# RWKV passes in another order, and norm rates kept per token on 128x8

## The reference

```python
    kk = heads(k * k_k)
    kk = kk * lax.rsqrt(jnp.sum(kk * kk, axis=-1, keepdims=True) + 1e-12)
    k = k * (1 + (a - 1) * k_a)
    rh, kh, vh, ah = heads(r), heads(k), heads(v), heads(a)
    decay = jnp.exp(-jnp.exp(heads(w_raw)))

    y = _rwkv7_scan(rh, decay, kh, vh, -kk, kk * ah)
    y = _layer_norm(y, gn_g, gn_b, GN_EPS)
    bonus = jnp.sum(rh * kh * r_k.astype(jnp.float32), axis=-1, keepdims=True) * vh
    y = (y + bonus).reshape(Bsz, T, D_B).astype(p_b.dtype)
    return y * jax.nn.silu(gate)
```

## Time and profile before

| what | us |
|---|---|
| median of 3 runs | 2367.26 (2361.62 to 2368.75) |
| the profiled execution, its own time | 2364.19 |
| its span, from first to last instruction | 2362.5 |
| of which passes 0 to 3 of the RWKV branch | 234.2 to 440.8 |
| PE busy | 2154.4 (91%) |
| DVE busy | 1347.4 (57%) |
| ACT busy | 789.4 (33%) |
| POOL busy | 620.1 (26%) |
| mean granted TensorE clock | 0.962 of full speed |

### The profile page before, as it was taken

One profiled execution on the slowest core, in us unless ns is written; L12 is line 12 of the kernel. 1 busy time (PEld: TensorE's weight loads), 2 busy tenths in 40 slices (PEclk: granted clock), 3 DMA queues, 4 the chain that ended last, 5 costly groups with the idle time before them and its releaser, 6 DMA issues.

```text
span 2362.5 us, 39580 instructions
## 1 busy us (share of the span) xinstructions
PE 2154.4 (91%) x15562; PEld 1559.1 (66%) x15562; DVE 1347.4 (57%) x2348; ACT 789.4 (33%) x1433; POOL 620.1 (26%) x1126
## 2 busy tenths in 40 slices
PE   4998787789998999999989968999998999999996
PEld 4876666565564555555555536888786778888875
DVE  2166666347997444444459986888785333333344
ACT  1334433223111344444310036545454432322223
POOL 0453211040102888888701121111111000000001
PEclk7999899899999999999999978999999999999998
DMA  7321323232444111111116433888886323333320
GB/s 292 99 89 63 109 110 144 110 107 79 159 168 144 44 66 56 50 50 61 57 66 239 164 110 118 247 248 237 249 246 210 96 84 98 98 98 98 98 90 36
DMA packets 105000, 294.56 MB, mean 125 GB/s; under 512 B 12400, under 2 KB 49520, under 8 KB 96240
## 3 DMA queue, kind: packets, MB, share of 16 engines
q1 hardware_dynamic: 92464, 227.02, 29.6%
q0 software_dynamic: 12352, 65.02, 7.3%
HBM read 225.01 MB, written 66.98 MB: 124 GB/s over the span
## 4 chain that ended last, share of the span: by engine, by line
PE 80%; DVE 6%; DMA 6%; ACT 3%; issue 3%; SPq 1%; POOL 0%; ACTq 0%; DVEq 0%; POOLq 0%
PE psum L449 29%; PE psum L1706 7%; PE psum L2358 7%; PE psum L2140 4%; PE psum L2105 4%; PE psum L2522 4%; DMA lags<-const 3%; PE psum L2116 2%; PE psum L1006 2%; PE psum L2183 2%; PE psum L2176 2%; PE psum L2129 2%; PE psum L2716 2%; PE psum L2662 1%; PE psum L283 1%
## 5 line engine op out<-in xcount | busy, mean ns | idle before, releaser
L449 PE MATMUL psum<-split,w_split 128*128 128x512 f32 x1632 | 373.2, 390 | 3.7 <-DVE w_split L431 3.7
L449 PEld LDWEIGHTS psum<-split,w_split 128*128 128x128 f32 x1632 | 307.5, 189 | 68.1 <-DVE w_split L431 4.1
L431 DVE TENSOR_TENSOR w_split<-ring,w_split 128x512 fp32r<-128x512 f32 x188 | 133.1, 708 | 318.5 <-ACT w_split L426 318.2
L1925 POOL TENSOR_TENSOR early<-early 128x8 f32<-128x8 f32 (+6 forms) x672 | 277.1, 412 | 52.8
L426 ACT ACTIVATE w_split<-ring 128x512 fp32r<-128x512 f32 x188 | 118.8, 632 | 349.0 <-PE psum L449 345.7
L1706 PE MATMUL psum<-early,ring 128*128 128x512 f32 (+1 forms) x544 | 176.6, 486 | 0.0
L2358 PE MATMUL psum<-gate,ring 128*128 128x512 f32 (+1 forms) x512 | 165.4, 486 | 1.2 <-issue 1.2
L2522 PE MATMUL psum<-h,u_w 128*128 128x256 f32 (+1 forms) x768 | 149.9, 349 | 14.4 <-ACT u_t L2444 13.7
L449 PE MATMUL psum<-h,w_split 128*128 128x512 f32 x624 | 147.9, 398 | 8.5 <-DVE w_split L431 8.5
L1706 PEld LDWEIGHTS psum<-early,ring 128*128 128x128 f32 x544 | 103.7, 191 | 71.8 <-issue 64.6
L2358 PEld LDWEIGHTS psum<-gate,ring 128*128 128x128 f32 x512 | 97.2, 190 | 69.3 <-issue 62.7
(11 more groups left out here) (413 smaller groups left out, 3709.5 us busy)
## 6 DMA issues: line engine op xcount, KB each, us to landing
ring<-in_s_glu SPq DMA_DIRECT2D x64, 512.0 KB, 3.5
ring<-in_w_mod SPq DMA_DIRECT2D x48, 512.0 KB, 5.2
made_c_pow<-area POOLq DMA_DIRECT2D x16, 1152.0 KB, 5.0
c_pow<-made_c_pow SPq DMA_DIRECT2D x16, 1152.0 KB, 6.6
made_b_pow<-area POOLq DMA_DIRECT2D x16, 1024.0 KB, 4.6
b_pow<-made_b_pow SPq DMA_DIRECT2D x16, 1024.0 KB, 10.2
ring<-in_s_in SPq DMA_DIRECT2D x32, 512.0 KB, 6.6
ring<-in_w_in SPq DMA_DIRECT2D x29, 512.0 KB, 3.5
```

The costliest lines, as they stand in the source:

```text
L431: nc.vector.tensor_tensor(rounded(buffer(u, 1)), source(u), buffer(u, 0), ALU.subtract).then_inc(dve_done, 1)
L449: ins = nc.tensor.matmul(out, rounded(buffer(u, w)[:, ks]), values(x, k), start=(first and k == 0 and n == 0), stop=(last and k == UNIT_K ...
L1925: nc.gpsimd.tensor_tensor(o, a, b, op).then_inc(pool_done, 1)
```

## The change

It has two parts. First, both rates are formed per token. `head_sums_pe` takes the squares as the stationary operand, 128 tokens at a time, and two columns of `block_ones` as the moving one, so that the sums lie with tokens on partitions, 128x8 for all tokens and both heads of a pair. Square root and reciprocal work on 128x8 (`key_rate`, `gn_rate`). `spread_pe` brings the rate back to 64 channels of each head by eight products, with the rate's column broadcast as the stationary operand and the identity as the moving one; DVE reads the result from PSUM. This is done once for each of the four pairs and for each of the two norms.

Second, instructions stand elsewhere. On PE the EARLY rows of a pass's first batch come ahead of the AKT product; the keys' sums come after the first level of U, ahead of the first `dz_pe`; state 3 too; the keys' spread stands where the keys' sums stood; the group norm's spread comes after `chunk_maps_pe`, ahead of the third batch. On ACT the keys' square no longer waits for AKT (the sigmoid now writes `be_cm` and leaves `a_cm`), the keys' root comes ahead of the second level's copies, the group norm's square ahead of a copy of `tm`, and the third batch's copy ahead of the gain. On DVE the bonus products (`prep_rk_dve`) come ahead of the keys, the addition of the first batch ahead of the third level's additions to Z, the first half of the operands ahead of the fourth level's, the small reciprocal of the group norm between `r_read` and `carry`, and `gn_out_dve` moves from the end of a pass to the second level of the next, for pair 2 into `rwkv_last_dve`, behind the fourth split of `mixT`.

```diff
@@ project_pe
                 if job == WD_JOB + 3:
                     prep_k_ss_pe(pe, 0)
+                if job == WD_JOB + 4:
+                    prep_k_spread_pe(pe, 0)
@@ project_dve
                 if FIRST_RAW + p == WD_JOB + 2:
-                    prep_recip_dve(dve, 0, 0)
-                    prep_recip_dve(dve, 0, 1)
+                    prep_rk_dve(dve, 0)
+                    prep_recip_dve(dve, 0)
                     prep_keys_dve(dve, 0)
-                    prep_rk_dve(dve, 0)
@@ new helpers
+        def head_sums_pe(out, src):
+            for tt in range(TT):
+                ins = nc.tensor.matmul(out[:, 2 * tt:2 * tt + 2], src[:, tt * P:(tt + 1) * P], mask("block_ones")[:, 0:P:HEAD],
+                                       start=True, stop=True)
+            return ins
+        def spread_pe(out, rate):
+            for tt in range(TT):
+                for e in range(2):
+                    ins = nc.tensor.matmul(out[half(e), tt * P:(tt + 1) * P],
+                                           rate[:, 2 * tt + e:2 * tt + e + 1].broadcast_to([P, HEAD]), mask("ident"),
+                                           start=True, stop=True)
+            return ins
+        def prep_k_spread_pe(pe, q):
+            pe.wait_ge(*at("rw", q, "k_rate"))
+            spread_pe(bank(6), key_rate[:, 1, :]).then_inc(pe_done, 1)
@@ prep_k_sq_act
-            if q > 0:
-                act.wait_ge(*at("rw", q - 1, "AKT"))
@@ prep_norm_act
-            nc.scalar.activation(kk[:, :], bank(6), ACT.Sqrt, bias=eps[:, 3:4]).then_inc(act_done, 1)
+            nc.scalar.activation(key_rate[:, 0, :], bank(6, 0, 2 * TT), ACT.Sqrt, bias=eps[:, 3:4]).then_inc(act_done, 1)
@@ prep_recip_dve
-            nc.vector.reciprocal(tmp[:, hs], kk[:, hs]).then_inc(dve_done, 1)
+            nc.vector.reciprocal(key_rate[:, 1, :], key_rate[:, 0, :]).then_inc(dve_done, 1)
@@ gn_spread_pe (new), gn_rate_dve (new), gn_scale_dve
+            pe.wait_ge(*at("gn", q, "rate"))
+            spread_pe(bank(4), gn_rate[:, 1, :]).then_inc(pe_done, 1)
+            nc.vector.reciprocal(gn_rate[:, 1, :], gn_rate[:, 0, :]).then_inc(dve_done, 1)
-            nc.vector.reciprocal(gn_rcp[:, :], gn_std[:, :]).then_inc(dve_done, 1)
-            nc.vector.tensor_tensor(y, y, gn_rcp[:, :], ALU.mult).then_inc(dve_done, 1)
+            nc.vector.tensor_tensor(y, y, bank(4), ALU.mult).then_inc(dve_done, 1)
@@ rwkv_last_dve
             for k in range(4):
                 split_dve(dve, "mix_split", mix_split, mixT, k)
+            gn_out_dve(dve, q - 1)
```

More of the change, by code:

```diff
@@ L834, in prep_k_ss_pe @@
             pe.wait_ge(*at("rw", q, "decay_sig"))
-            nc.tensor.matmul(bank(6), mask("block_ones"), tmp[:, :], start=True, stop=True).then_inc(pe_done, 1)
+            head_sums_pe(bank(6), tmp).then_inc(pe_done, 1)
             pe_count.up("rw", q, "k_ss")
+        def prep_k_spread_pe(pe, q):
+            pe.wait_ge(*at("rw", q, "k_rate"))
+            spread_pe(bank(6), key_rate[:, 1, :]).then_inc(pe_done, 1)
+            pe_count.up("rw", q, "k_spread")
         def prep_rk_sum_pe(pe, q):
@@ L904, in prep_scan_dve @@
             dve.wait_ge(*at("rw", q, "decay_sig"))
[L905 removed]
+            nc.vector.tensor_tensor_scan(g_cm[:, :], reset, be_cm[:, :], 0.0, ALU.mult, ALU.add).then_inc(dve_done, 1)
             dve.wait_ge(dve_done, dve_count.up("rw", q, "scanned"))
         def prep_decays_dve(dve, q):
[L909 removed]
+            nc.vector.tensor_tensor(a_cm[:, :], g_cm[:, :], be_cm[:, :], ALU.subtract).then_inc(dve_done, 1)
             dve_count.up()
@@ L1231, in gn_ss_pe, with gn_spread_pe @@
             pe.wait_ge(*at("gn", q, "sq"))
-            nc.tensor.matmul(bank(5), mask("block_ones"), gn_sq[:, :], start=True, stop=True).then_inc(pe_done, 1)
+            head_sums_pe(bank(5), gn_sq).then_inc(pe_done, 1)
             pe_count.up("gn", q, "ss")
+        def gn_spread_pe(pe, q):
+            pe.wait_ge(*at("gn", q, "rate"))
+            spread_pe(bank(4), gn_rate[:, 1, :]).then_inc(pe_done, 1)
+            pe_count.up("gn", q, "spread")
         def gn_centre_dve(dve, q):
@@ L1326, in rwkv_pe @@
                 prep_raw_pe(pe, i + 1)
+            vec_rows_pe(pe, n0, EARLY, *([("vec", n0 - 1, "added")] if n0 > FIRST_GATE else []))
             akt_pe(pe, i)
@@ L1330, in rwkv_pe @@
             u_pe(pe, i, 1)
-            vec_rows_pe(pe, n0, EARLY, *([("vec", n0 - 1, "added")] if n0 > FIRST_GATE else []))
-            dz_pe(pe, i, 1)
+            if prep:
+                prep_k_ss_pe(pe, i + 1)
             if scan:
                 state_pe(pe, i - 1, 3)
+            dz_pe(pe, i, 1)
             vec_rows_pe(pe, n0, LATE)
@@ L1383, in rwkv_act @@
             u_act_(act, i, 1)
+            if prep:
+                prep_norm_act(act, i + 1)
             u_act_(act, i, 2)
             vec_copy_act(act, batches[0])
-            if prep:
-                prep_norm_act(act, i + 1)
             u_act_(act, i, 3)
@@ L1400, in rwkv_act @@
             w_act_(act, i)
-            if prep:
-                prep_tm_act(act, i + 1, 1)
             if scan:
@@ L1405, in rwkv_act @@
             if prep:
+                prep_tm_act(act, i + 1, 1)
                 prep_tm_act(act, i + 1, 2)
@@ L1411, in rwkv_act @@
                 prep_tm_act(act, i + 1, 3)
+            if len(batches) == 3:
+                vec_copy_act(act, batches[2])
             if scan:
                 gn_gain_act(act, i - 1)
-            if len(batches) == 3:
-                vec_copy_act(act, batches[2])
             if i == 0:
@@ L1433, in rwkv_dve @@
                 prep_decays_dve(dve, i + 1)
+            if prep:
+                prep_recip_dve(dve, i + 1)
+            if i > 1:
+                gn_out_dve(dve, i - 2)
             dz_dve(dve, i, 2)
@@ L1465, in rwkv_dve @@
                 gn_scale_dve(dve, i - 1)
-                gn_out_dve(dve, i - 1)
             if len(batches) == 3:
```

57 lines of the change are left out of this document (31 added, 26 removed).

## The result

The changed kernel takes 2340.44 us (median of 4 runs, 2338.34 to 2342.94), the kernel before 2365.38 us (4 runs, the three of the table above and one more). The ratio is 0.9893, with a 95% interval of 0.9874 to 0.9911. The forecast was 2342.2. A second set gave 2339.02 against 2363.60, ratio 0.9888 (0.9866 to 0.9911).

The account below looks back on a forecast made before the run. No engine was taken as full: a pass is a chain through all, its lateness showing as PE waits. Terms -1.4 - 3.0 - 12.3 - 3.9 + 1.7 - 1.7 - 1.4 = -22.0 took 2364.2 to 2342.2 us, range 2332 to 2355.

Parts of the forecast that it names:

- Step 1: End of the projections: two bonus products done while the keys wait for their spread, -1.4 us (bounds 0 and -3.4).
- Step 2: Pass start to second level: ACT's square early, EARLY rows moved into mask waits, -4.2; spreads +1.2; together -3.0 us.
- Step 3: Second to fifth level: PE's waits on vector additions, `tmp`, operands and ahead of y end, -12.3 us (bound -8).
- Step 4: Ends of passes 1 and 2: earlier row copy -5.9, earlier square -1.0, two spreads +3.0; together -3.9 us.
- Step 5: End of pass 3 and tail: tail rows start earlier, -1.2; `gn_out_dve` of pair 2 delays states, +1.4; together +1.7 us.
- Step 6: Last group norm, whose end PE waits for: 3.35 us reciprocal goes, 0.17 and a 1.5 spread come; -1.7 us.
- Step 7: TensorE's clock: pass 1 at 0.94 instead of 0.88 would be 2.9 us shorter; half taken, -1.4 us.
- signs of being wrong: Wrong if PE's AKT, weight or `issue` waits grow over 5 us, a spread exceeds 3, projections' DVE end stays 227.8.
- Rival one: Passes: new waits for weights and where rows run into products take back a third, +9 us, 2351; chance 0.18.
- Rival two: Passes: more gain, clock staying up (7 us) and spreads overlapping, -10.5 us, 2332; chance 0.12.
- Rivals three and five: Three: spread far dearer, +38, 2380, chance 0.03; five: weight stream paces passes, only Step 1 and Step 6 left, 2361, 0.04.
- rival four: Spreads: each new change of array mode costs the last product's length, 12 changes, +2.4 us, 2344.6; chance 0.05.

Follow-up runs that it names:

- rates alone: Kernel before with its old instruction order, both rates on 128x8 and spread; 2348.3 us, ratio 0.9904.
- AKT wait back: Changed kernel with one wait put back: ACT's square of the keys waits for AKT as before; 2346.6 us, ratio 0.9927.
- EARLY rows back: Changed kernel with the EARLY rows of a pass's first batch behind the keys' sums, ahead of the first `dz_pe`; 2337.7 us, ratio 0.9875.
- order alone: Kernel before with every engine's instructions in the new order, both rates at full size, no spread; 2338.6 us, ratio 0.9882.
- second profile: Profile of the changed kernel run once more without an edit; median 2339.0 us, ratio 0.9888, profiled execution 2330.8 us.

## Why the prediction was right

The median came within 2 us of the forecast, the profiled execution within 4, and this is partly luck. The change was put at 22.0 us; it is 24.9 by the medians and 25.9 between the two profiles. The terms it had for the waits held, but errors larger than this difference cancelled around them. Gains of some 16 us were missing: 8.6 of clock, 4.7 of waits for masks, and 3 because seven spreads took 1.03 us instead of 1.5. Losses of 12 us were missing too: 5.7 for weights, 2.7 of `issue`, and 3.6 in parts of the program that were not changed.

- **Step 1** (-1.4): the profile shows -1.3. In the ten kernels with short rates and the new order, the stretch from the last two jobs to pass 0 is 49.4 to 51.3 us, in the three with full rates 52.5 to 52.7. The rates alone, short but in the old order, have 52.2, so it is the new place of the bonus products that gains, as argued. The reasoning held; the size lies between 1 and 3.
- **Step 2** (-3.0): the 4.7 us on UA are gone, and AKT wait back shows them as 6.5 us where they would now fall. What the step left out is that the EARLY rows, put into mask waits of 7.0 us, take 4.7 of them (1.1 and 1.2 remain) and cost 5.7 for weights; EARLY rows back shows that this nets to about nothing. The spread is 1.03, not 1.5.
- **Step 3** (-12.3): the waits named, 12.3 us in all, are down to 0.2 (operands). Right; the order does most of it, as the 2.1 of operands and 3.0 ahead of y show, which the rates alone kept.
- **Step 4** (-3.9): the turns wait 0.4 us a pass, the square fell from 2.8 to 1.6 us. Right in size; that the new place of the copy was needed was wrong, since the short reciprocal alone does it, or the place alone.
- **Step 5** (+1.7): of the 3.7 us that PE no longer waits for at the end of pass 3 (4.1 less 0.4), 2.6 came back as a later weight, and `gn_out_dve` cost 1.4 (1.3 came back when it moved). Both as argued.
- **Step 6** (-1.7): from the group norm's square to the long run it was 11.5 us (469.85 to 481.35) and is 9.0 (445.31 to 454.31): -2.5, the sums and the spread being cheaper. The order alone kept 11.5 (447.18 to 458.67), the rates alone have 9.0 (466.30 to 475.30), so this is the short rate's.

```profile
469.85 0.63 ACT L1243 ACTIVATE gn_sq<-rkvg 128x512 f32<-128x512 f32 x1 [2.19 <-DVE rkvg L1238]
...
481.35 2.08 PE L449 MATMUL psum<-mix_split,out_w 128*128 128x512 f32 x4 [8.91 <-DVE mix_split L467]
```

```profile
445.31 0.63 ACT L1270 ACTIVATE gn_sq<-rkvg 128x512 f32<-128x512 f32 x1 [2.19 <-DVE rkvg L1265]
...
454.31 4.21 PE L449 MATMUL psum<-mix_split,out_w 128*128 128x512 f32 x9 [4.68 <-DVE mix_split L467]
```

- **Step 7** (-1.4) is the term that was mis-sized. The busy time of each pass at the clock it had, against the same instructions at 1.00 in the order alone (35.88, 39.91 twice, 34.65), puts 12.9 us of the kernel before on the clock; in the changed kernel some 3 are left (1.5 in pass 0, against 36.12 at 1.00 in its second profile, and about as much in pass 3). So the clock gave about 10 us, by one profile of each kernel. I had taken half of one pass, though the earlier trace rows show three others at 0.93 and 0.94.

Of the forecast's own signs of being wrong, one showed: the waits for weights grew by more than 5 us (5.7; 4.5 in the second profile). Together with AKT's masks (7.0 to 2.3) and `issue` (2.7 more) the growth is 3.7. The end of the projections is later by the clock of the profile (228.86 against 227.86), but it stands 44.7 us behind the start of the last two jobs, and stood 46.2 behind it.

Rival one's losses came nearly whole in size: 5.7 us of weights where it had 3.9, and 2.7 us more `issue` where it had 5.2, together 8.4 of its 9. But its reading of `issue`, that rows run straight into products, is wrong. Even the stall of before that it rests on comes 99 matmul records after the start of the products, in their fourth group:

```profile
284.74 1.02 PE L992 MATMUL psum<-rkvg,k_cm 64*64 64x64 f32 x27 [2.59 <-issue]
```

The eight stalls of the changed kernel stand in all four passes, in the midst of products, and each of them stands at the same instruction in the second profile, which has two more. Counted from the program's start over all of PE's instructions in the trace (products, weight loads and semaphore waits), 4546, 5057, 5826, 7617, 8130, 8898, 10690 and 11458 instructions stand before them: the distances are multiples of 256, give or take one. The same holds for all 122 stalls of over 0.2 us that the 14 profiles put down to `issue` in the passes and the tail: divided by 256, their counts leave 193 or 194 (one 196). With every spread issued twice, the stalls moved to other instructions and kept such counts. So how many instructions came before matters, and not what stands there. Not every possible place stalls, and the sum runs from 4.8 to 12.7 us per profile. What PE waits for at these places no row names.

Rival two's gains came too, the clock and the overlap. I had given the two rivals chances as alternatives, and both happened at once. Rivals three and five are out: a spread is 1.03 us, and the passes shortened while the DMA share rose to 0.28 to 0.41. For rival four, the spread issued twice between 64x64 products leaves 0.17 us for start and end together, where it had 0.2 for each change. The Trainium skill (TensorEngine Tiling (Array Packing), Key Properties) states a drain at a change of mode; if there is one here, it is within that 0.17.

The windows forecast for the passes, 41, 48, 47 and 45, came as 42.0, 45.0, 47.0 and 43.5.

## What to carry to other kernels

When a chain of waits is cut in a stage where TensorE's granted clock is below 1.00, cost the clock too: take the busy time of the same instructions at a stretch with 1.00 in the profile, for every pass that is below it, not only the worst. Here it was a third of the gain in the passes. This gives what there is to win; whether a pass then gets the higher clock differs from one profile to the next, so it belongs in the range as well as in the sum.

A reciprocal per token instead of per channel can pay only where someone waits for it. In the last group norm it took 2.5 us off the way to the output projection. For the keys, and for the group norms of the passes, the experiments show no gain that can be told once the order is right, while each spread is 1.03 us of work on the busiest engine. So try the order first, by itself. And before giving an in-order engine a transfer to wait for, look at what stands behind it: two moved lines on ACT and DVE were worth 4.5 us in the tail.

## What was not expected of the hardware

Sixteen PE instructions (eight products) with a 128x64 stationary operand take 1.51 us if neighbours use the same half of the array and 1.03 if they alternate. Head sums by a stationary operand of squares and two moving columns cost 0.95 to 1.05 us for eight instructions, no more than the one wide product they replace (1.12). The reciprocal takes 3.35 us on 512 columns and 0.20 on 8.

PE's stalls without a named cause in these stages come 256 of its instructions or a multiple of it apart, give or take a few, in every profile: 122 of 122.

Identical instructions behind the tail took 1866.6 to 1883.6 us in the profiles of this study, more than most edits moved. Two things account for it: PE was busy for 1766 to 1775 us, as the granted clock there was 0.98 or 0.97, and it waited 8.0 to 10.8 us for the `lags` transfers, or not at all. What is left is 98.6 to 100.2 us in all 14.
